# Where the buffers start in SBUF: a two-block transformer kernel with its activation arena and its weight ring moved to rounder addresses

## The reference: what is computed

```python
h = h + hybrid_mixer(rmsnorm(h, norm_mix), w_in, b_f, conv_w, out_gain, w_out)
h = h + (silu(n @ w_gate) * (n @ w_up)) @ w_down          # n = rmsnorm(h, norm_ffn), 2048 -> 5632 -> 2048
x = rmsnorm(h, final_norm)[:, 16:]
...
x = x + gt1 * (concat([o_mla, o_na, o_fn]) @ w_out_2)     # second block, 256 tokens + 256 context tokens in w_in_2
u = conv3(n2 @ w_up_2)                                    # 2048 -> 11264
x = x + gt2 * (silu(u_gate) * u_val) @ w_down_2           # 5632 -> 2048
return rmsnorm(x, g_final)
```

## Time and profile before

| what | value |
|---|---|
| median of 3 runs | 2350.54 us (2350.31 to 2382.15) |
| the profiled execution | 2354.1 us |
| its span, first to last instruction | 2352.1 us |
| TensorE busy | 2342.0 us, 100% of the span |
| granted TensorE clock, mean | 1.00 |
| DVE, ACT busy | 1663.2 us (71%), 1123.4 us (48%) |
| moved by DMA | 509.19 MB, mean 216 GB/s |

### The profile page before, as it was taken

The page is one execution under the profiler, slowest core; times in us unless marked ns, Lnnn a source line. Parts: engine busy times, 40 slices in busy tenths (PEclk is TensorE's granted clock), DMA queues, the critical chain, the costliest instruction groups (busy, mean ns, idle before and its releaser), DMA issues.

```text
span 2352.1 us, 49789 instructions
## 1 busy us (share of the span) xinstructions
PE 2342.0 (100%) x19292; PEld 2279.5 (97%) x19292; DVE 1663.2 (71%) x2501; ACT 1123.4 (48%) x1500; POOL 0.2 (0%) x4
## 2 busy tenths in 40 slices
PE   9999999999999999999999999999999999999998
PEld 9998899999999999999988989799999999999998
DVE  6676678788877878888887755456666566655675
ACT  6354445544445554445632332455555355544554
POOL 0000000000000000000000000000000000000000
PEclk9999999999999999999999999999999999999999
DMA  7875566588778887787657722054565665666664
GB/s 284 285 272 195 188 233 233 198 285 303 273 255 283 280 285 240 264 290 270 224 200 258 258 80 93 22 175 166 192 196 194 194 191 187 199 193 191 197 192 143
DMA packets 141889, 509.19 MB, mean 216 GB/s; under 512 B 15824, under 2 KB 17360, under 8 KB 141392
## 3 DMA queue, kind: packets, MB, share of 16 engines
q1 hardware_dynamic: 141776, 507.60, 64.1%
HBM read 505.44 MB, written 2.10 MB: 216 GB/s over the span
## 4 chain that ended last, share of the span: by engine, by line
PE 99%; DVE 0%; DMA 0%; ACT 0%; SPq 0%; issue 0%; ACTq 0%
PE ps L1175 30%; PE ps L1177 30%; PE ps L1176 30%; PE ps L1517 1%; PE ps L1203 1%; PE ps L1205 1%; PE ps L1204 1%; PE ps L1535 1%; PE ps L1349 1%; PE ps L1526 0%; PE ps L1330 0%; PE ps L1374 0%; PE ps L1583 0%; PE ps L1355 0%; DMA raw<-in_stream 0%; PE ps L1331 0%
## 5 line engine op out<-in xcount | busy, mean ns | idle before, releaser
L1717 DVE TENSOR_TENSOR lo<-raw,hi 128x1024 fp32r<-128x1024 f32 x753 | 918.4, 1222 | 489.4 <-ACT hi L584 485.1
L584 ACT ACTIVATE hi<-raw 128x1024 fp32r<-128x1024 f32 x753 | 797.0, 1061 | 969.3 <-PE ps L1177 864.0
L1175 PE MATMUL ps<-hs,hi 128*128 128x256 f32 (+1 forms) x3056 | 860.7, 282 | 0.4 <-DVE hs L2526 0.3
L1176 PE MATMUL ps<-hs,hi 128*128 128x256 f32 (+1 forms) x3056 | 859.8, 281 | 0.0
L1177 PE MATMUL ps<-hs,lo 128*128 128x256 f32 (+1 forms) x3056 | 859.8, 281 | 0.0
L1176 PEld LDWEIGHTS ps<-hs,hi 128*128 128x128 f32 x3056 | 576.2, 189 | 5.0
L1175 PEld LDWEIGHTS ps<-hs,hi 128*128 128x128 f32 x3056 | 573.7, 188 | 6.2 <-DVE hs L2526 0.8
L1177 PEld LDWEIGHTS ps<-hs,lo 128*128 128x128 f32 x3056 | 573.7, 188 | 5.1
L1175 PE MATMUL ps<-hid,hi 128*128 128x256 f32 x1408 | 388.7, 276 | 0.0
L1176 PE MATMUL ps<-hid,hi 128*128 128x256 f32 x1408 | 388.6, 276 | 0.0
L1177 PE MATMUL ps<-hid,lo 128*128 128x256 f32 x1408 | 388.6, 276 | 0.0
(11 more groups left out here) (323 smaller groups left out, 2537.2 us busy)
## 6 DMA issues: line engine op xcount, KB each, us to landing
raw<-in_stream SPq DMA_DIRECT2D x753, 512.0 KB, 4.3
wm<-in_mod_stream SPq DMA_DIRECT2D x192, 512.0 KB, 4.8
out_tokens<-y_final SPq DMA_DIRECT2D x4, 512.0 KB, 3.7
h<-in_tokens SPq DMA_DIRECT2D x3, 544.0 KB, 8.7
cx<-in_ctx_tokens SPq DMA_DIRECT2D x6, 256.0 KB, 6.0
cbx<-in_c_rows SPq DMA_DIRECT2D x1, 1024.0 KB, 8.0
cbc<-in_c_rows SPq DMA_DIRECT2D x1, 1024.0 KB, 5.5
na<-in_na_bias SPq DMA_DIRECT2D x1, 1024.0 KB, 4.8
```

The costliest lines, as they stand in the source:

```text
L584: act.activation(hi[:, slot, :], raw[:, slot, :], ACT.Copy).then_inc(hi_done, 1)
L1175: pe.matmul(acc_, hi[:, slot, w], x_hi, start=kt == 0, stop=False)
L1176: pe.matmul(acc_, hi[:, slot, w], x_lo, start=False, stop=False)
L1717: dve.tensor_tensor(lo[:, slot, :], raw[:, slot, :], hi[:, slot, :].bitcast(F32), ALU.subtract)\
```

## The change

Nothing is computed otherwise, and no instruction is added, taken away or moved: each engine has the same instructions in the same order, with other addresses in them. What moves is memory:

- `mod`, `modx`, `gm` and `att` (384, 128, 192 and 192 bytes with their padding, 896 together) are placed ahead of the ring. The ring then starts at 17,408, a multiple of 1,024, and so do `hi` (33,792), `lo` (50,176), `wm`, `cbx` and `h`.
- `mp` and `pick` share one slot of 64 bytes, `pick` 32 bytes into it.
- `arena` is rounded up to a multiple of 256: 124,672, which is 768 beyond a multiple of 1,024. Rows of `hs`, `hid`, `hu` and the `ys` buffers now start at a multiple of 256; those of `xs1` still step by 1,088 bytes, from remainder 0 on. `std`, `rstd` and the work slab move from 64 beyond a multiple of 256 to a multiple; `tabs` moves from a multiple of 256 to 128 beyond one.

```diff
+        mod, _ = keep("mod", [P, MOD_TILES])
+        modx, _ = keep("modx", [P, CTX_TILES])
+        gm, _ = keep("gm", [P, 3, KT])
+        att, _ = keep("att", [P, 3, 2 * HEADS])
         raw, _ = keep("raw", [P, RING, CW])
         hi, _ = keep("hi", [P, RING, CW], F32R)
         lo, _ = keep("lo", [P, RING, CW], F32R)
...
         tabs, _ = keep("tabs", [P, N_TABS])
-        mod, _ = keep("mod", [P, MOD_TILES])
-        modx, _ = keep("modx", [P, CTX_TILES])
-        mp, _ = keep("mp", [P, 3, 2])
-        gm, _ = keep("gm", [P, 3, KT])
-        pick, _ = keep("pick", [P, HEADS], F32R)
-        att, _ = keep("att", [P, 3, 2 * HEADS])
+        _, o_mp = keep("mp_pick", [P, 16])
+        mp = at("mp", [P, 3, 2], F32, o_mp)
+        pick = at("pick", [P, HEADS], F32R, o_mp + 32)
         cq, _ = keep("cq", [P, 2, HEADS])
...
-        arena = top[0]
+        arena = -(-top[0] // 256) * 256
```

## The result

The changed kernel takes 2439.94 us (median of 4; 2439.65 to 2440.44), the kernel before 2351.35 us in the same series: slower, by a ratio of 1.0335 with a 95% interval of 1.027 to 1.040. The executions of the kernel before fall into two groups, near 2351 and near 2380 us. The ratio takes in both; against the first group alone, at 2351, it is 2439.94 / 2351 = 1.038.

A forecast was written before the change was run, and what follows sets the result against it. The prediction took TensorE's matmul count times pitch as the bound. Its terms summed to 0, from -28.7 to +53.6 us, on the median of 2350.5 us, so it forecast 2350.5 us, range 2316 to 2378.

The forecast's parts named there:

- What bounds the kernel: Whole kernel: time is the number of TensorE matmuls times their pitch, about 113.3 ns low or 117.7 ns high.
- The traffic, ACT, DVE: DMAs and the ring's writers on ACT and DVE might get quicker or slower, hidden by the ring: -1 to +1 us.
- the small buffers: `mod`, `modx`, `gm`, `att`, `mp`, `pick`, in short operations beside the matmuls: nothing, with 0.2 us either way.
- The cover of 4.3 us a chunk: Ring slack: four slots last 10.9 us against 6.6 us from DMA issue to `lo`, leaving 4.3 us a chunk.
- What tells the two pitches apart is not an address: First feed-forward, parts a and b: same addresses, 113.3 and 117.7 ns, so a TensorE pipeline state set by short groups.
- the arena and the ring: Starts of moving rows and weight blocks in all large matmuls: rounding them most likely changes the time by 0 us.
- The upper bound: All low-pitch 256-column matmuls go to the high pitch, 11,904 x 4.4 = 52.4 us; whole sum up to +53.6 us.
- The lower bound: Most the whole change could save: -28.7 us, of which -27.5 for rounder starts.
- B: Rival: the high pitch needs an unrounded start and vanishes, giving 2337 us, or 2323 with `xs1`; chance 0.20.
- Rival D: Slower: moving row and weight block both start at multiples of 256, keeping the high pitch; 2356 to 2403 us, chance 0.15.
- C: Rival: a lower pitch for every float32r matmul with round starts; chance 0.11, of which 0.09 beyond 2%.
- `xs1` comes nearest: Query projection rows passing through remainder 0 run at 116.7 ns, above the low pitch, so a 0 start alone buys nothing.

The follow-up runs named there:

- b_settle: Kernel before with four added groups of two 128-column float32 matmuls on TensorE, products unread: 2358.91 us, ratio 0.9988.
- r64_a0: Changed kernel with only `gm` ahead of the ring, so ring 64 beyond a multiple of 256, arena at a multiple: 2353.70 us, ratio 0.9966.
- r0_a192: Changed kernel with the arena 192 beyond a multiple of 256, ring still at a multiple of 1,024: median 2364.57 us, ratio 1.0023.
- lo_shift: Kernel before's ring and arena remainders, with buffer `lo` alone moved on by 64 bytes: 2413.72 us.
- r128_a96: Ring as in the kernel before, arena moved to 96 beyond a multiple of 256: 2414.20 us, one execution.
- r128_a32: Ring as in the kernel before, arena moved to 32 beyond a multiple of 256: 2412.10 us, one execution.
- flip_block2: Kernel before with one added group of two 128-column float32 matmuls behind the first layer of block two's feed-forward: 2379.29 us.

## Why the prediction was wrong, point by point

- **What bounds the kernel** was right: TensorE's pitch, and nothing else, made the change, with TensorE busy for 100% of the span at a granted clock of 1.00 before and after. The traffic, ACT, DVE and the small buffers were rightly put at nothing: an operation of the ring's writers takes 1058 ns on ACT for 1061 and 1223 on DVE for 1222, a chunk's DMA lands in 4.2 us for 4.3 (medians, 753 chunks). A chunk lasted as reckoned: in block one ACT's conversions start 2.72 us apart before (999.54, 1002.26 and 1004.98 us) and 2.88 after (564.66, 567.54 and 570.42), which is 24 x 120.0 ns. The cover of 4.3 us a chunk was an estimate from medians; what the traces show of it is that ACT waited for the ring's DMAs 23 times in 753 chunks before and 17 times after.
- **"What tells the two pitches apart is not an address"** was right for parts a and b, and misleading as a step. That a state chooses between two pitches at one set of addresses says nothing about other addresses, where neither of the two need exist. That it is a state of a pipeline of weight loads and matmuls was my inference: the rows show where the pitch turns, no run shows what holds it. Nor does a 128-column group always take the high pitch out: it put it in in b_settle.
- **The step that failed** is in *the arena and the ring*: "neither 64 against 128 on the moving side nor on the weight side moves it ... I take 0 us as the likeliest, since the row nearest to the new case ... shows no difference". I compared remainders one by one, where the distance between them counts. Turned round, the kernel's operands go from distance 192 to 64, the only other one at which the low pitch has been seen: that both gave 113.3 ns was chance, and I read it as indifference. The new case was distance 0, of which I wrote "no row has both at 0", and priced it by rows at other distances.
- **The upper bound**, +53.6 us, took the high pitch as the worst that could happen, and the stated range ended at 2378 us, below it. There is a third level at 120.0 ns, 2.3 above it, and it took every 256-column row of constant start: +85.4 us. A level seen in a trace is no bound for a case that isn't in it.
- **The lower bound**, -28.7 us, had -27.5 for rounder starts. 13.5 of them are the high pitch, 3,072 matmuls (1,536 in part b's up projection, 768 in each output projection) x 4.4 ns. The other 14.0, which also take B from 2337 to 2323, were the rows of `xs1`, brought down to pitches that no run shows: those rows run at 125.0 ns after for 126.4 (272 columns), 120.7 for 120.7 (258) and 118.7 for 118.1 (256).
- **Rival D** named the sign and the relation that counts, the one between the two operands, with 0.15. The mechanism it gave isn't shown, and "in step" isn't the whole of it, for distance 96 costs as much as 0. Its price of 4.4 ns a matmul was 6.7, its "spread from 2356 to 2403" assumed that only some stretches turn, and all did. Its argument against, that "the distance between the starts differed too", had the right quantity and drew the wrong conclusion from two values of it.
- **Rivals B and C** fell. B: the high pitch needs no start off a multiple of 256 on either side, as part b of r64_a0 (150.0 / 1274 = 117.7 ns, arena at 0) and block one of r0_a192 (117.8, ring at 0) show; it did vanish after the change, but upwards. C (0.11, of which 0.09 beyond 2%) was a lower pitch for every float32r matmul with round starts. No run shows the floor it was reckoned from: r64_a0 stays at 113.3 ns with the arena at a multiple of 256, and no stretch of 256 float32r columns came below 113.1.
- **"`xs1` comes nearest"** misread those rows: they have two distances in each triple of matmuls, since x_hi and x_lo start 1,088 bytes apart, and the one other kernel with unlike distances in a triple was high too (lo_shift, 118.2 ns). They hardly changed with the arena (118.1 to 118.7 ns for 256 columns) and so couldn't tell what a constant one would do. Their 116.7 was the count of too short a window; it lay above the low pitch all the same, so the argument drawn from it doesn't change.
- **Steps of 64 bytes, and a line more for each row**, which the expectations of r128_a96 and r128_a32 weighed, don't account for this case: no run shows such a line. Measured, moving the arena by 32 bytes changes the pitch (117.8 or 113.3 to 118.2 ns, distance 192 to 224), and the four arenas off a multiple of 64 ran at 116.7 to 119.9 ns in most layers, no slower than the 120.0 of distance 0.

What stays open: why a distance costs what it does, what the high pitch is, and what an interruption does to it. My guess is the weight load, which the trace shows under each matmul (PEld is busy 2368.8 of the 2437.5 us beside PE, with as many loads as matmuls, 19,292), and which would read SBUF in step with the moving row; that is argued from the table by distance, not shown, since no run took the loads away. If nothing tied the two reads together, a distance between the two starts should cost nothing; here it adds up to 6.7 ns to 113.3, for float32r with a new weight block for each matmul. Where the two meet, no run shows.

## What to carry to other kernels

Where TensorE is the bound and every matmul loads new float32r weights, measure the start-to-start time of matmuls against their columns, and then move one operand's buffer by 64, 128 and 192 bytes against the other: that is one line, and it moved this kernel by 89 us. Round addresses were no aim in themselves here; what counted was the start of the moving row against that of the stationary block, modulo 256 (113.3 ns at 192, 120.0 at 0), the same for all operands of a chain (118.2 ns in lo_shift, where one of three differs). No version here beat the kernel before; its distance of 192 was the best of the eight tried.

## What the hardware showed that I hadn't expected

- Distance between moving and stationary start, at 256 float32r columns: from 113.3 ns (192, and 64 in `by_token`) to 120.0 ns (0, 96), with values between that don't run in order. Columns matter: 512 of them run at 226.4 ns at distance 0 and 233.8 at 192, the other way round.
- Two pitches at one distance, 113.3 and 117.7 ns at 192, each held for hundreds of microseconds (from 1645 us to the end of block two's feed-forward, 113.1 to 113.4 in every window of the kernel before and 117.6 to 117.8 in flip_block2); also 118.6 and 120.0 at 128, and 117.3, 118.6 and 120.0 at 160. With block two's 6,144 matmuls in one or the other the kernel takes near 2351 or near 2380 us (6,144 x 4.4 ns = 27 us): two groups of executions of the same program at a granted clock of 1.00.
- At distance 0 there is one pitch alone, and all four executions agree within 0.8 us. The slower layout is the steadier one.
